# A decoder step on one core: the modulation product in blocks of 512 columns, and most of it moved behind the first projection

## The reference, cut to what matters

```python
def modulations(c, li):
    mod = jax.nn.silu(c) @ w_ada[li] + b_ada[li]
    return jnp.split(mod[:, None, :], 6, axis=-1)

def post_norm(x, sub, gate, li, j):
    return layer_norm(ALPHA * x + (1.0 + gate) * sub, ln_g[li, j], ln_b[li, j])

for li in range(DEPTH):                                  # DEPTH = 2
    up = xp * (1.0 + mod_p[1]) + mod_p[0]                # shift and scale before the mixer
    ...                                                  # mixer: attention + mLSTM (layer 0), RG-LRU (layer 1)
    xp = post_norm(xp, yp, mod_p[2], li, 0)              # gate behind the mixer
    up = xp * (1.0 + mod_p[4]) + mod_p[3]
    xp = post_norm(xp, ffn(up, li), mod_p[5], li, 1)
```

## Time and profile before

| | us |
|---|---|
| three runs | 1695.06, 1696.95, 1705.46 |
| median | 1696.95 |
| the profiled execution, its own time | 1704.68 |
| its span, first to last instruction | 1702.9 |
| granted TensorE clock, mean over the span | 0.908 |
| bytes moved by DMA | 175.03 MB, mean 103 GB/s |
| TensorE busy, share of the span | 89% |
| VectorE busy, share of the span | 47% |

### The profile page before, as it was taken

One profiled execution on the slowest core, in us unless ns is written; L12 is line 12 of the kernel. 1 busy time (PEld: TensorE's weight loads), 2 busy tenths in 40 slices (PEclk: granted clock), 3 DMA queues, 4 the chain that ended last, 5 costly groups with the idle time before them and its releaser, 6 DMA issues.

```text
span 1702.9 us, 27896 instructions
## 1 busy us (share of the span) xinstructions
PE 1509.6 (89%) x11536; PEld 1394.8 (82%) x11536; DVE 803.8 (47%) x1196; ACT 501.9 (29%) x623; POOL 260.3 (15%) x202
## 2 busy tenths in 40 slices
PE   5979998998677969999999968797878999999995
PEld 2569995655367869999999958797877999999994
DVE  1173323776655473323233477658766333333345
ACT  0031114332311342221222235475225221122222
POOL 2000001000203510000000441453341000000043
PEclk9989996777566989999999979998989999999996
DMA  9943226433641213124321320231341323432211
GB/s 327 348 156 100 73 77 222 148 126 103 182 141 25 75 50 96 54 86 124 100 83 52 122 66 26 75 105 32 87 126 42 83 68 94 124 92 67 69 35 50
DMA packets 240037, 175.03 MB, mean 103 GB/s; under 512 B 8887, under 2 KB 233772, under 8 KB 239796
## 3 DMA queue, kind: packets, MB, share of 16 engines
q1 hardware_dynamic: 237952, 169.70, 32.9%
q0 software_dynamic: 1840, 3.79, 0.8%
q10 hardware_dynamic: 140, 0.09, 0.0%
HBM read 168.00 MB, written 5.63 MB: 102 GB/s over the span
## 4 chain that ended last, share of the span: by engine, by line
PE 71%; DVE 16%; DMA 4%; issue 4%; ACT 3%; SPq 2%; POOL 1%; DVEq 0%; ACTq 0%; POOLq 0%
PE ps L2030 54%; PE ps L2049 6%; DMA raw<-in_w_ada 3%; PE ps L2104 2%; DVE wlo L1461 2%; PE ps L1975 2%; DVE nb L1572 1%; PE ps L2175 1%; DVE xc L1706 1%; DVE UL L1565 1%; PE ps L1861 1%; DVE rstd L1628 1%; DVE cmB L1241 1%; PE ps L2115 1%; DVE ub L1583 1%
## 5 line engine op out<-in xcount | busy, mean ns | idle before, releaser
L2030 PE MATMUL ps<-UH,whi 128*128 128x260 f32 x1936 | 392.8, 284 | 12.9 <-DVE wlo L1461 12.9
L2030 PE MATMUL ps<-UH,wlo 128*128 128x260 f32 x1936 | 392.6, 285 | 0.0
L2030 PE MATMUL ps<-UL,whi 128*128 128x260 f32 x1936 | 392.0, 284 | 0.0
L926 ACT ACTIVATE whi<-raw 128x2048 fp32r<-128x2048 f32 (+3 forms) x115 | 193.9, 1686 | 634.1 <-PE ps L2030 513.0
L2030 PEld LDWEIGHTS ps<-UH,whi 128*128 128x128 f32 x1936 | 300.9, 190 | 14.2 <-DVE wlo L1461 14.2
L2030 PEld LDWEIGHTS ps<-UH,wlo 128*128 128x128 f32 x1936 | 301.0, 190 | 0.0
L1461 DVE TENSOR_TENSOR wlo<-raw,whi 128x2048 fp32r<-128x2048 f32 (+3 forms) x115 | 253.8, 2207 | 99.7 <-ACT whi L926 99.1
L2030 PEld LDWEIGHTS ps<-UL,whi 128*128 128x128 f32 x1936 | 299.8, 190 | 0.0
L1639 DVE TENSOR_TENSOR hb<-ps,silb 128x520 f32<-128x520 f32 x44 | 30.8, 700 | 281.6 <-PE ps L2030 260.6
L2030 PE MATMUL ps<-HH,whi 128*128 128x260 f32 x616 | 124.1, 283 | 0.0
L2030 PE MATMUL ps<-HH,wlo 128*128 128x260 f32 x616 | 123.8, 283 | 0.0
(11 more groups left out here) (423 smaller groups left out, 2164.6 us busy)
## 6 DMA issues: line engine op xcount, KB each, us to landing
raw<-in_w_ada SPq DMA_DIRECT2D x96, 512.0 KB, 7.2
raw<-in_w_ffn_in SPq DMA_DIRECT2D x88, 512.0 KB, 4.9
raw<-in_w_in_even SPq DMA_DIRECT2D x24, 512.0 KB, 4.8
raw<-in_w_ffn_out SPq DMA_DIRECT2D x32, 384.0 KB, 3.9
raw<-in_w_ffn_out SPq DMA_DIRECT2D x32, 320.0 KB, 3.2
raw<-in_w_in_odd SPq DMA_DIRECT2D x20, 512.0 KB, 4.5
raw<-in_w_out_odd SPq DMA_DIRECT2D x16, 320.0 KB, 3.6
raw<-in_w_out_even SPq DMA_DIRECT2D x8, 512.0 KB, 3.9
```

The costliest lines, as they stand in the source:

```text
L926: ins = nc.scalar.activation(whi[w % 2][:, 0:f], raw[c % NRAW][:, 0:f], ACT.Identity)
L2030: ins = T.matmul(ps(g)[:, hf, 0:HT], wt[:, k, wc], x[:, k, hf], start=(k == 0 and wt is wh and x is xh), stop=(k == s.k - 1 and wt is wl_))
```

## The change

The modulation is made in 24 blocks of 512 columns (`NBLK`), 12 per layer, and a block is two chunks of 512 rows by 512 columns (1 MB each, `e` = 0, 1, with four row tiles each). In a block each of the four column groups of the array takes a 128-column piece of its own and sums over all 1024 rows: 32 products of 128 columns per block. PSUM then holds 128 finished columns on each strip, VectorE copies 128x128 and not 128x256, and one turning product with 36 columns, with a selection matrix per strip, turns all four strips at once. Rows of a DMA are 2 KB long where they were 1 KB.

Only the first 4 blocks (`FIRST`, shift and scale of layer 0, 8 chunks) stay ahead of the projection. The other 20 (`adaB`, 40 chunks) stand in the middle: 4 beside the transposes of `kv`, none beside `bkv`, and 16 in the steps 0 to 15. The sums of scale and shift are cut into `scale_and_shift` and `gate_plus_one`; ahead of the projection only `scale_and_shift(0)` is left, and the rest stands where `modulation_sums(1)` stood. In a step VectorE takes `block_rows(d)` and then `block_select(d - 1)` last, where it took `select` of an older chunk just behind `scores`. A raw buffer that held the first half of a block is free on `half_done`.

```diff
-STEPS, ADA_EARLY = 18, 6
+STEPS, NBLK, FIRST, EARLY = 18, 24, 4, 4
...
-            c[32 * j + r, C_ADA + r] = 1.0
+            c[32 * j + r, C_ADA + 9 * j + r] = 1.0
...
-    stage("ada0", 24, 8, 256, 2)
+    stage("ada0", 2 * FIRST, 4, 512, 0)
...
-    stage("ada1", 24, 8, 256, 0)
...
+    stage("adaB", 2 * (NBLK - FIRST), 4, 512, 0)
+    for i in range(EARLY):
+        one(("kv", i), ("mod", FIRST + i))
+        if i >= 1:
+            one(("sel", FIRST + i - 1))
...
-        modrow = am("modrow", [P, 2, 256], 56192)
+        modrow = am("modrow", [P, 2, P], 56192)
...
-                wait_filled(sp, mod_use(t, old - t.c0))
+                d = block_of(t, old - t.c0)
+                if (old - t.c0) % 2 == 0:
+                    sp.wait_ge(half_done, d + 1)
+                else:
+                    wait_filled(sp, use[("mod", d)])
...
             for s_ in range(STEPS):
                 h, quarter = s_ // 4, s_ % 4
-                c = ADA_EARLY + s_
+                d = FIRST + EARLY + s_
                 if s_ < 16:
                     scores(s_)
-                if s_ >= 1:
-                    select(ada, c - 2)
                 if 1 <= s_ < 17:
                     weights(s_ - 1)
...
-                modulation_rows(ada, c)
-            lo(ada.c0 + ada.n)
-            lo(ada.c0 + ada.n + 1)
+                if d < NBLK:
+                    block_rows(d)
+                if d <= NBLK:
+                    block_select(d - 1)
+            lo(st["eout"].c0)
+            lo(st["eout"].c0 + 1)
...
-            select(ada, 22)
-            select(ada, 23)
-
...
-            modulation_sums(1)
+            gate_plus_one(0, 0)
+            scale_and_shift(1)
+            gate_plus_one(0, 1)
+            for j in range(2):
+                scale_and_shift(2 + j)
+                gate_plus_one(1, j)
...
+            def block_rows(d):
+
+                g = use[("mod", d)]
                 wait_filled(dve, g)
-                free(v.tensor_copy(modrow[:, c % 2], ps(g)[:, 0, 0:256]), g)
+                free(v.tensor_copy(modrow[:, d % 2], ps(g)[:, 0, 0:P]), g)
...
+            for d in range(FIRST):
+                block_rows(d)
+                if d >= 1:
+                    block_select(d - 1)
+            block_select(FIRST - 1)
+            lo(st["ein"].c0)
+            lo(st["ein"].c0 + 1)
             setup_dve()
-            modulation_sums(0)
+            scale_and_shift(0)
...
                 if s_ >= 2:
                     pv(s_ - 2)
-                mod_products(ada, ADA_EARLY + s_)
+                d = FIRST + EARLY + s_
+                if d < NBLK:
+                    block_products(d)
                 if s_ < 15:
                     scores(s_ + 1)
                 if 1 <= s_ < 17:
                     transposes(s_ - 1)
-                mod_select(ada, ADA_EARLY + s_ - 1)
-            mod_select(ada, 23)
+                if d <= NBLK:
+                    block_turn(d - 1)
...
+            def block_products(d):
+
+                g = use[("mod", d)]
+                begin(g)
+                s = st["ada0" if d < FIRST else "adaB"]
+                for e in range(2):
+                    gc = s.c0 + 2 * (d - (0 if d < FIRST else FIRST)) + e
+                    pe.wait_ge(raw_loaded[gc % NRAW], 32 * (gc // NRAW + 1))
+                    for k in range(4):
+                        for j in range(4):
+                            w0 = k * 512 + j * P
+                            ins = T.matmul(ps(g)[32 * j:32 * j + 32, 0, 0:P], cF[:, 4 * e + k], raw[gc % NRAW][:, w0:w0 + P],
+                                           start=(e == 0 and k == 0), stop=(e == 1 and k == 3))
+                    if e == 0:
+                        ins.then_inc(half_done, 1)
                 done(ins)
...
+            def block_turn(d):
+
+                g = use[("sel", d)]
+                begin(g)
+                gm = use[("mod", d)]
+                pe.wait_ge(freed[gm % NGRP], gm // NGRP + 1)
+                done(T.matmul(ps(g)[:, 0, 0:36], modrow[:, d % 2], cn[:, C_ADA:C_ADA + 36], start=True, stop=True))
```

More of the change, by code:

```diff
@@ L184, in trunk, with block_of @@
     st, use, order = plan()
[L186 to L193, removed]
+    def block_of(s, c):
+        return c // 2 + (FIRST if s.name == "adaB" else 0)
     chunk_stage = {}
@@ L454, in weight_view @@
             if n[:3] == "ada":
-                return a["w_ada"][int(n[3])].rearrange("(k p) (c m) -> c p k m", p=P, m=256)
+                both = [a["w_ada"][l].rearrange("(e k p) (c m) -> c e p k m", e=2, p=P, m=512) for l in range(2)]
+                return [both[block_of(s, c) // 12][block_of(s, c) % 12][c % 2] for c in range(s.n)]
             if n == "ein":
@@ L1549, in _, with part, gate_plus_one @@
-            for c in range(24):
-                modulation_rows(st["ada0"], c)
-                if c >= 1:
-                    select(st["ada0"], c - 1)
-            select(st["ada0"], 23)
-            lo(24)
-            lo(25)
+            def part(q, i):
+                l, j = q // 2, q % 2
+                return modT[l][:, (3 * j + i) * 8:(3 * j + i + 1) * 8]
+            def gate_plus_one(l, j):
+                gt = part(2 * l + j, 2)
+                link(v.tensor_scalar(gt, gt, 1.0, None, ALU.add))
@@ new lines, in scale_and_shift @@
+            def scale_and_shift(q):
+                r = q - 1
+                link(v.tensor_scalar(G9[:, q], part(q, 1), 1.0, None, ALU.add))
+                if r < 0:
+                    link(v.tensor_copy(B9[:, q], part(q, 0)))
+                else:
+                    lb = lnT[:, :, 4 + r:5 + r].broadcast_to([P, KD, 9])
+                    lg = lnT[:, :, r:r + 1].broadcast_to([P, KD, 9])
+                    link(v.tensor_tensor(B9[:, q], G9[:, q], lb, ALU.mult))
+                    link(v.tensor_tensor(B9[:, q], B9[:, q], part(q, 0), ALU.add))
+                    link(v.tensor_tensor(G9[:, q], G9[:, q], lg, ALU.mult))
@@ L1798, in middle_pe @@
             pe.wait_ge(evac, 24)
-            ada = st["ada1"]
             for tb in range(4):
```

122 lines of the change are left out of this document (36 added, 86 removed).

## The result

The changed kernel took 1647.1 us (median of 4 runs, 1644.64 to 1648.48) where the kernel before took 1701.2 (4 runs) beside it: ratio 0.9688, 95% interval 0.9661 to 0.9714. The profiled span is 1644.6 us for 1702.9.

What follows compares the result with a forecast made beforehand. Taken as bounds: the weight stream in the front, TensorE and the engines' order in the middle. Terms -51.8 - 1 + 22 - 0.5 = -31.3 took the profiled 1704.68 to 1673.4, or 1666 as median; range 1648 to 1690.

Steps and rivals of the forecast that it cites:

- The front: Ahead of the projection: 16 chunks leave, six sums leave the chain, longer DMA rows load faster; -51.8 us.
- the six sums: Ahead of the projection: six of eight small sums leave the chain, 6 x 0.24 = -1.5 us.
- The 2 KB rows: In the front: the 8 chunks that stay load faster in longer rows; -2.0 us, ends 0 and -3.8.
- The transposes: Beside the key and value transposes: eight chunks for six, cheaper turnings against a DMA wait; -1 us, ends -2 and +4.
- The wait for block 7: Beside the transposes: its two chunks can be issued only when block 5 is used, at 3.0 us each.
- The steps: In the middle's 16 steps: a second chunk each and a new wait for the turning; +22 us, bounds 8 and 38.
- the wait of `block_select`: At a step's end VectorE waits for the turning, with the next scores queued behind; 0.35 to 0.65 us a step.
- the second chunk: In each of 16 steps: its 16 products add 1.75 us at clock 0.50 and 0.9 at 1.00.
- the third rival: In the steps: more products hold the clock at 1.00, steps cost 8 us or less, time 1650; chance 14%.
- Behind the last head: After the steps: VectorE's two splits can start earlier, behind the last outputs; -2.0 us.
- The sums behind: Behind the steps: sums ahead of line 1291 grow from 10 to 16, 6 x 0.24 = +1.5 us.
- The other rivals: Weight loads exposed behind halved products, 1707 to 1713, chance 6%; block loads late in the steps, 1682, chance 13%.

Runs made afterwards that it cites:

- the 1 KB run: Changed kernel with every block's load cut into two halves of its columns, so rows are 1 KB long; 1653.24 us, ratio 0.9715.
- the kernel in the old form: Changed kernel with 256-column chunks, 1 KB rows, four turning products and a 512-column copy a block, so the move without the new form; 1672.14 us, ratio 0.9836.

## Why the prediction was right and wrong

In profiled spans the change gave 58.3 and 58.4 us in its two profiles; 31.3 were worked out. In medians it was 54 and 52: the profiled execution of before, from which the sum was made, was a long one. Stage by stage, in the first profile: the front -52.6, the projection -0.4, the transposes -4.3, the steps +3.1, behind the last head -5.4, the sums behind +1.5.

**The front (-51.8): right, measured -52.6.** The projection's second chunk lands 51.1 earlier, for 50.3 (16 chunks and the faster rows). From its landing to the first product it was 15.38 us and is 13.88: -1.5, as worked out for the six sums. The 2 KB rows, -2.0 between bounds, were measured with the 1 KB run: 2.0. The estimate by the Trainium skill's limit of 358 GB/s (DMA: Bandwidth & Descriptors, Specifications), -0.7, was too small; the 385 and 391 GB/s of the 2 KB rows disagree with that limit.

**The transposes (-1, ends -2 and +4): the wait was right, the size uncertain.** The stretch is -4.3 and -2.4 in the two profiles of the change, beyond the lower end, and -1.8, -1.6, +0.2 and +0.7 in four other kernels with the same code there. With the first head it is -3.5 and -3.6 in the two profiles of the change; that head alone was priced at +7. The wait for block 7, the fourth beside the transposes, was named there and stands in every profile of a kernel of the new form that makes it there, from 1.38 to 3.16 us with 2 KB rows; the kernel in the old form has none.

**The steps (+22, bounds 8 and 38): this step failed.** Measured +3.1 and +1.2. One part of it was right, the wait of `block_select` (6 to 8 us in total). The other, the second chunk at 0.9 to 1.75 us a step, assumed that each step would keep the clock that the earlier trace rows show. It was the third rival, the clock that stays up, that came true in the main (0.81 to 0.90 in the heads, not 1.00), at 1650 for 1647. Even the bound of 8 was too high, since it priced only what was added at the high clock: the scores, sums and transposes that were there already got shorter too (scores 428 ns for 538). The doubled products in the old kernel show it by themselves (-2.9 for the heads where the price was 14 to 28), and the products added to the changed kernel show its limit (+36). That the time lies no more than 0.9 below the range is luck: the gain of 54.1 lies 4.5 beyond the sum's lower end, and the median from which the range was counted, 1696.95, lies 4.2 below the one measured beside the change.

**Behind the last head (-2.0): too small, -5.4.** The two splits moved as named. But the last two steps, which lie in this stretch, also lost their two chunks and turnings, and I put a second chunk into 16 steps without taking the old one out of two. One block in step 16 costs 1.8 there. How much of the other 3.4 the two chunks made is not shown.

**The sums behind (+1.5): right, +1.50.**

**The other rivals.** The weight loads never came out of hiding. The loads were late beside the transposes and nowhere in the steps: from 200 to 365 us TensorE's products wait 1.7 us for `w_ada` (last figures of the row: idle before, and for what), the 0.31 and 1.38 shown ahead of the heads.

```profile
L2115 PE MATMUL ps<-raw,cF 128*32 128x128 f32 x1280 | 47.2, 309 | 1.7 <-DMA raw<-in_w_ada 1.7
```

## What to carry to other kernels

Before adding products to a stretch where TensorE runs below its full clock, price them twice, with all TensorE work of the stretch at either level; the cheapest test is to issue the products that are there twice and look at the clock and at the busy time. Where the clock is near full already, added products cost their length. An evacuation that waits for the step's last TensorE work belongs behind the next step's first vector work, not ahead of it: here that and one early block moved late were worth another 10 us.

## What was not expected of the hardware

TensorE's busy time fell when it was given more to do: 117.1 us in the heads with one chunk a step, 110.8 with the same chunk twice. The busy share doesn't tell the clock's level either: in the first head of before TensorE was busy for all 26.54 us at 0.55, and with the products doubled for 21.06 of 24.52 at 0.93. What in these products raises the clock stays open; the move in the old form had as many product columns per step and clocks of 0.78 to 0.87 only, so their number alone doesn't settle it.
